# Sums of squares of the recurrent queries: products with a column of ones in place of transposes

## What is computed

```python
def l2_normalize(t):
    tf = t.astype(jnp.float32)
    return tf * lax.rsqrt(jnp.sum(tf * tf, axis=-1, keepdims=True) + RMS_EPS)

dq = l2_normalize(dq.reshape(B, S, DN_HEADS, DN_HEAD_DIM))
dk = l2_normalize(dk.reshape(B, S, DN_HEADS, DN_HEAD_DIM))
o_dn = gated_delta_rule(dq, dk, dv, beta, g)      # chunks of 64 positions
```

## Time and profile before

| | before |
|---|---|
| median of 3 runs | 1422.45 us (1422.43 to 1423.66) |
| profiled execution | 1423.01 us |
| its span in the trace | 1421.2 us |
| granted TensorE clock, mean | 0.998 |
| TensorE busy | 1401.3 us (99%) |
| VectorE busy | 980.7 us (69%) |
| ScalarE busy | 575.4 us (40%) |
| GpSimd busy | 270.2 us (19%) |

### The profile page before, as it was taken

One profiled execution on the slowest core, in us unless ns is written; L12 is line 12 of the kernel. 1 busy time (PEld: TensorE's weight loads), 2 busy tenths in 40 slices (PEclk: granted clock), 3 DMA queues, 4 the chain that ended last, 5 costly groups with the idle time before them and its releaser, 6 DMA issues.

```text
span 1421.2 us, 22312 instructions
## 1 busy us (share of the span) xinstructions
PE 1401.3 (99%) x8474; PEld 1151.7 (81%) x8474; DVE 980.7 (69%) x1788; ACT 575.4 (40%) x1254; POOL 270.2 (19%) x293
## 2 busy tenths in 40 slices
PE   8999999999999999999999999999999999999997
PEld 7788887888888888778888888888888788888885
DVE  6999844666666666365528797666674777777778
ACT  4655532323332332342203355555544544444540
POOL 4332234423333243233910000000000000000000
PEclk9999999999999999999999999999999999999999
DMA  6233352443244422234442144433345975555422
GB/s 210 90 119 111 112 192 86 122 118 108 76 109 112 119 68 84 71 108 160 158 189 89 60 163 163 163 142 133 136 161 186 339 222 179 163 164 187 128 70 119
DMA packets 114134, 195.01 MB, mean 137 GB/s; under 512 B 27696, under 2 KB 59504, under 8 KB 111728
## 3 DMA queue, kind: packets, MB, share of 16 engines
q1 hardware_dynamic: 105104, 174.21, 37.1%
q10 hardware_dynamic: 8928, 19.40, 3.6%
HBM read 135.84 MB, written 57.74 MB: 136 GB/s over the span
## 4 chain that ended last, share of the span: by engine, by line
PE 90%; DVE 6%; DMA 1%; ACT 1%; issue 1%; SPq 0%; ACTq 0%; DVEq 0%
PE ps L2070 16%; PE ps L2445 6%; PE ps L2447 6%; PE ps L2446 6%; PE ps L1963 6%; PE ps L1965 6%; PE ps L1964 6%; PE ps L2429 5%; PE ps L2428 5%; PE ps L2430 5%; PE ps L2138 4%; PE ps L2023 3%; PE ps L2025 3%; PE ps L2024 3%; PE ps L2078 2%; PE ps L2219 1%
## 5 line engine op out<-in xcount | busy, mean ns | idle before, releaser
L2445 PE MATMUL ps<-thi,shi 128*128 128x512 f32 x416 | 162.0, 389 | 0.8 <-DVE tlow L1854 0.7
L2447 PE MATMUL ps<-thi,slow 128*128 128x512 f32 x416 | 161.9, 389 | 0.0
L2446 PE MATMUL ps<-tlow,shi 128*128 128x512 f32 x416 | 161.8, 389 | 0.0
L2070 PE MATMUL ps<-xh,ring2l 128*128 128x512 f32 x304 | 124.6, 410 | 0.0
L2070 PE MATMUL ps<-xl,ring2h 128*128 128x512 f32 x304 | 123.6, 406 | 0.0
L2070 PE MATMUL ps<-xh,ring2h 128*128 128x512 f32 x304 | 122.4, 402 | 0.0
L860 ACT ACTIVATE thi<-b 128x512 fp32r<-128x512 f32 x104 | 65.5, 630 | 110.1 <-PE ps L2447 109.4
L1854 DVE TENSOR_TENSOR tlow<-b,thi 128x512 fp32r<-128x512 f32 x104 | 71.9, 691 | 53.4 <-ACT thi L860 53.4
L760 POOL TENSOR_TENSOR ring2l<-raw,ring2h 128x256 fp32r<-128x256 f32 x116 | 92.2, 823 | 2.3
L2445 PEld LDWEIGHTS ps<-thi,shi 128*128 128x128 f32 x416 | 78.1, 188 | 17.6 <-DVE slow L1847 1.1
L2447 PEld LDWEIGHTS ps<-thi,slow 128*128 128x128 f32 x416 | 78.1, 188 | 16.4
(11 more groups left out here) (430 smaller groups left out, 3573.6 us busy)
## 6 DMA issues: line engine op xcount, KB each, us to landing
raw<-in_wblk SPq DMA_DIRECT2D x55, 512.0 KB, 3.6
sraw<-hpark SPq DMA_DIRECT2D x104, 256.0 KB, 2.8
hpark<-hq SPq DMA_DIRECT2D x16, 1024.0 KB, 4.6
b<-in_wblk SPq DMA_DIRECT2D x64, 256.0 KB, 3.4
wraw<-in_wblk SPq DMA_DIRECT2D x30, 512.0 KB, 3.8
hpark<-hq SPq DMA_DIRECT2D x16, 768.0 KB, 4.9
park<-ub ACTq DMA_DIRECT2D x40, 256.0 KB, 2.0
park<-cacc ACTq DMA_DIRECT2D x12, 512.0 KB, 3.3
```

What stands on the lines that cost most here:

```text
L2070: ins = mm(ps[h][:, :], w, x_, start=(r == 0), stop=(r == 23))
L2445: mm(outp, shi[s][:, ts], thi[m][:, :], start=first, stop=False, skip_group_check=True)
L2446: mm(outp, shi[s][:, ts], tlow[m][:, :], start=False, stop=False, skip_group_check=True)
L2447: return mm(outp, slow[s][:, ts], thi[m][:, :], start=False, stop=final, skip_group_check=True)
```

## The change

The squares are made first, in `dqs` itself, by one ScalarE instruction over 128x512 elements (`a_qsq`), which signals a new semaphore `qsq_ok`. TensorE then multiplies the squares of each head, as weights, with one column of ones. The result is the sum over channels for 128 positions, one column of `C0` per head. ScalarE copies these four columns into `ssa`. `a_trq` keeps its name and its place in TensorE's list, and waits for `qsq_ok` in place of `dn_in`.

```diff
             def a_squares_q(t):
 
                 act.wait_ge(trq_mm, t + 1)
-                for h in range(NH):
-                    ins = act.activation(sqj[:, h, :], C0h[:, h, :], ACT.Square, accum_out=ssa[:, h:h + 1])
-                ins.then_inc(sqq_ok, 1)
+                cp(ssa[:, 0:NH], C0[:, 0:NH]).then_inc(sqq_ok, 1)
+
+            def a_qsq(t):
+
+                act.wait_ge(dn_in, 48 * t + 48)
+                act.activation(dqs[:, :, :], dqs[:, :, :], ACT.Square).then_inc(qsq_ok, 1)
 
@@ ScalarE's step @@
                 if t is not None: b_exps(t, 1)
                 if n is not None: a_exps(n)
+                if n is not None: a_qsq(n)
                 if t is not None: b_osq(t)
@@ ScalarE ahead of the first step @@
             a_eg(0)
             a_exps(0)
+            a_qsq(0)
             a_squares_q(0)
@@ TensorE @@
             def a_trq(t):
-                pe.wait_ge(dn_in, 48 * t + 48)
+                pe.wait_ge(qsq_ok, t + 1)
                 if not isinstance(t, int) or t >= 2:
                     pe.wait_ge(on_ok, t - 1)
-                trans(C0h, lambda h: dqs[:, h, :]).then_inc(trq_mm, 1)
+                for h in range(NH):
+                    last = mm(C0[:, h:h + 1], dqs[:, h, :], ones[:, 0:1], start=True, stop=True)
+                last.then_inc(trq_mm, 1)
```

More of the change, by code:

```diff
@@ L374, in hybrid_block @@
         sqq_ok = sem("sqq_ok")
+        qsq_ok = sem("qsq_ok")
         sqk_ok = sem("sqk_ok")
```

## The result

The changed kernel takes 1429.94 us (median of 6 runs, 1427.76 to 1433.45), the kernel before 1422.44 us (6 runs, 1420.66 to 1423.66). The ratio is 1.0052, interval 1.0042 to 1.0062: 6.0 to 8.8 us slower. The forecast was 1429.0 us, in a range of 1424.4 to 1432.1 us. The profiled execution took 1431.73 us, span 1429.9 us.

The account below looks back on a forecast made before the run. The prediction took TensorE's instruction list to bound the mixed stage. Products (3.8 us) plus the wait at tile 0 (2.7 us) added 6.5 us to 1422.45 us, forecast as 1429.0 us, range 1424.4 to 1432.1 us.

Parts of the forecast that it names:

- The bound: Mixed stage, 200 to 560 us: TensorE's instruction distances set its length; other engines' relief matters only for one 0.6 us wait.
- The price of the products: TensorE, every tile: eight pairs at 0.11 us replace four transposes, 0.45 to 0.53 us a tile, 3.8 us over 8 tiles.
- rival 1: TensorE's products: one column is cheap, 0.26 us a group; only tile 0's wait remains, +2.0 us, 1424.5 us; chance 0.13.
- The wait at tile 0: At a_trq(0) TensorE stands 2.7 us for ScalarE's square, queued behind a_eg(0) and a_exps(0); bounds 0 and 2.9 us.
- the cover: Steps: the square delays osb by at most 0.62 us, hidden by 3.5 us between its writing and TensorE's taking it.
- The clock: Behind tile 0's standstill: no lower clock expected, as the start's 4.2 us wait lies in a window at granted clock 1.00.
- Rival 5: Tile 0's standstill lowers the granted clock, some 2 us on top, 1431 us; chance 0.03.
- The sum: Whole kernel: 3.8 us for the products plus 2.7 us for tile 0's wait, 6.5 us slower.

Follow-up runs that it names:

- experiment 10: Changed kernel with tile 0's square earlier in ScalarE's list, squares and ones as float32r, two columns of ones: 1423.16 us, ratio 1.0004.
- experiment 2: Changed kernel with one line moved, so ScalarE squares dqs ahead of a_eg(0) at tile 0: 1425.94 us, ratio 1.0023.
- experiment 3: Kernel before, with transposes; at tile 0 ScalarE also squares dqs into scratch and TensorE's transposes wait for it: 1425.68 us, ratio 1.0025.
- experiment 9: Changed kernel with tile 0's square earlier in ScalarE's list and each head's product split in two of 64 positions: 1426.02 us, ratio 1.0019.
- Experiment 5: Changed kernel with 9 fills in place of 4 ahead of tile 0's products, 19 in place of 24 later: 1427.37 us, ratio 1.0034.
- Experiment 1: Changed kernel with 18 fills in place of 4 ahead of tile 0's products, 10 in place of 24 later: 1426.75 us, ratio 1.0029.
- experiment 7: Changed kernel with 128 columns of ones in place of one, ScalarE copying one column of each head's 128: 1430.33 us, ratio 1.0053.
- experiment 8: Changed kernel with each head's product split in two of 64 positions, 16 instructions a tile: 1429.34 us, ratio 1.0042.

## Why the prediction was right, and where it was not

**The bound.** TensorE's list, with its one old wait of 0.6 us, sets the end of the mixed stage. Shown: experiment 10 relieves ScalarE as the change does, keeps TensorE's list at its length, and changes nothing; experiments 2, 3 and 9 move the end by what they do to TensorE's list, within 0.15 us of the sum of its distances. Experiment 5 lies 0.05 us above such a sum. Experiment 1 lies 0.33 us above it, and 0.28 us of that stand in one place, behind tile 0's values: two fills there start 0.42 and 0.32 us behind the one before, at 214.16 and 214.48 us, in place of 0.23 us. The first follows the end of ScalarE's evacuation `ub` at 214.02 us, so it probably waited for its bank; the trace does not name the wait.

**The price of the products.** Forecast 0.45 to 0.53 us a tile, 3.8 us in all. Measured without the wait: 0.415 us a tile, 3.3 us in all. At tile 3 it is 0.80 - 0.43 = 0.37 us, and 0.03 us more behind the transposes of `osb` (343.11 to 343.50 us, 0.36 us before); where fills stand behind the products, as at tile 1, it is 0.80 - 0.36 = 0.44 us. The mechanism is the one named: two instructions of each kind per head, and a distance set by something that does not depend on the columns (experiment 7) and that falls with half the weights (8) or half the instructions (10). That this something is the weight load is the reading that fits all three; no row shows the load's own length apart from its latency. I took 0.11 us a pair and it was 0.10 us.

Of the two rules of the Trainium skill, "TensorE: Matmul & The Clock Gate", section on LDWEIGHTS, held: about 107 ns a load of 128 columns against 0.10 us measured. "TensorEngine Tiling (Array Packing)", section Instruction Overhead, gives products of one column about 60 cycles, and my estimate from it was 0.2 us a tile; the trace shows 0.80 us. That rule leaves the weight load out, and rival 1 fell with it.

**The wait at tile 0.** Forecast 2.7 us, measured 2.25 us, once, and not in the steps of tiles 1 to 7. The place and the chain were right. The size depends on VectorE: its first mask addition took 0.43 us in the changed kernel and 0.80 us in the profile of before, from whose ScalarE rows I took the start of the square. That is 0.37 us of the miss. The other 0.09 us are the square and the way to TensorE, 208.31 to 208.97 us on ScalarE's and TensorE's timelines, 0.66 us where I had 0.62 + 0.13 us. In experiment 3 the same addition took 1.01 us, 0.58 us more than in the changed kernel, and the standstill was 2.84 us, 0.59 us more. In the steps the square took some of the cover, as expected: VectorE's last write of `osb` starts at 339.45 us, takes 0.68 us, and TensorE takes `osb` at 343.11 us, so 3.0 us are left of 3.5 us.

**The clock.** This is the step that failed. Rival 5, with a chance of 0.03, is what happened in most executions, on top of the forecast. The forecast argued from a wait of 4.2 us at the start of the program under a granted clock of 1.00. That row did not carry over. It has no work of TensorE ahead of the wait, and it does not even show that the products behind the wait ran at full speed. Here are TensorE's products with `xraw` (line 1975) in the kernel before, first those that start between 4 and 9 us, then some from 14 to 17 us (count, duration in ns as min/median/max, first and last start):

```profile
L1975 PE MATMUL ps<-wavraw,xraw x16: 434/434/592, 4.2 to 8.3; 128*128 128x136 f32 x16
L1975 PE MATMUL ps<-wavraw,xraw x29: 279/279/279, 13.7 to 17.0; 128*128 128x136 f32 x29
```

The same product took 434 ns right behind the wait and 279 ns later, and starts lay 0.23 us apart in place of 0.12 us. That is about the ratio that the fills show at a granted clock of 0.50 in the changed kernel (0.42 in place of 0.23 us), but it stands beside a granted clock of 1.00 in the row. So before a granted clock of 1.00 is taken for full speed, the distances of equal instructions have to agree with it; in the mixed stage they do.

In the changed kernel the clock fell in both profiled executions, for 1.7 us and 3.4 us of loss. Its size had been named as some 2 us.

**The sum.** 3.8 + 2.7 = 6.5 us was forecast. In the stretch of the first profile it is 3.3 + 2.25 + 1.7 = 7.25 us, against 7.29 us measured. The forecast came near in part because two terms were a little too large (by 0.5 and 0.45 us) and one was left out (1.7 us). That they nearly cancelled is luck. The timed difference, 6.0 to 8.8 us, holds both sums. The 1.8 us between the profiled executions ahead of the mixed stage are not explained by the change; they come and go among executions of all kernels here, and I did not look for their cause.

Not tried: extra work for ScalarE in the steps, to find where its cover ends.

## What to carry to other kernels

A product with one column was no cheap reduction on TensorE here: with fresh weights it cost 0.10 us against 0.11 us with 128 columns, and a float32 head needed two of them. Before putting data in as weights to be summed, compare with what a transpose costs, which stands in the trace as one pair (0.09 to 0.11 us). And a new semaphore between engines must be checked in the prologue too: the steady steps had 8 us of cover, tile 0 had none, and one line moved in ScalarE's list was worth 4.0 us of the stretch, more than the whole price of the products (3.3 us).

## What the runs showed of the hardware

A standstill of TensorE of 2.25 to 3.81 us in dense work was followed, in five of six profiled executions, by 3.4 or 6.8 us at a granted clock of 0.50, which cost 1.7 or 3.4 us on top of the standstill; in the sixth, of 2.84 us, and in the one execution with 1.10 us, it was not. In the same kernel the length differed between executions. I had thought of a 2 us wait as costing 2 us. "TensorE: Matmul & The Clock Gate" in the Trainium skill says, under "What's actually happening", that the gate follows how busy the array has been recently; these rows agree, but do not show what decides between the five and the sixth.

A weight load and product of 128x128 with one column took 0.10 us, with 128 columns 0.11 us, with 64 columns of weights, results going to the two halves of the partitions in turn, 0.035 us each (and 0.09 us once ahead of the group), and in the form of the fills 0.09 us, but there one pair per head is enough.
